# Weights streamed through TensorE from their last column to their first, with the PSUM output in the same order

## The reference

```python
x = x + 0.5 * swiglu(rms_norm(x, norm_ffn1_w), ffn1_w_gate, ffn1_w_up, ffn1_w_down)   # D_FF = 5632
x = x + head_group_mixer(rms_norm(x, norm_mix_w), w_in, attn_sinks, ret_gn_w, w_out)  # D_IN = 5376
x = x + 0.5 * swiglu(rms_norm(x, norm_ffn2_w), ffn2_w_gate, ffn2_w_up, ffn2_w_down)
return rms_norm(x, norm_final_w)

def swiglu(h, w_gate, w_up, w_down):
    return (jax.nn.silu(h @ w_gate) * (h @ w_up)) @ w_down
```

## Time and profile before

| | us |
|---|---|
| median of 3 runs | 1844.76 |
| lowest and highest run | 1844.43, 1845.06 |
| the profiled execution, own time | 1844.38 |
| its span, first to last instruction | 1842.6 |

### The profile page before, as it was taken

One profiled execution on the slowest core, in us unless ns is written; L12 is line 12 of the kernel. 1 busy time (PEld: TensorE's weight loads), 2 busy tenths in 40 slices (PEclk: granted clock), 3 DMA queues, 4 the chain that ended last, 5 costly groups with the idle time before them and its releaser, 6 DMA issues.

```text
span 1842.6 us, 23062 instructions
## 1 busy us (share of the span) xinstructions
PE 1830.3 (99%) x8570; PEld 1537.5 (83%) x8570; DVE 1045.0 (57%) x1087; ACT 832.0 (45%) x996; POOL 63.3 (3%) x59
## 2 busy tenths in 40 slices
PE   9999999999999999999999999999999999999998
PEld 7888888888888888999998888888888888888886
DVE  5565465455556557555557665555555556546546
ACT  7444443444444444555555455444444444444344
POOL 0000000000000000000009000000000000000000
PEclk9999999999999999999999999999999999999999
DMA  9565555555555555555555456555556565565552
GB/s 367 195 194 186 193 190 186 197 185 191 195 183 187 200 183 172 179 179 167 172 160 180 137 182 206 183 190 197 183 192 193 184 195 190 187 195 188 190 198 92
DMA packets 177345, 346.61 MB, mean 188 GB/s; under 512 B 6048, under 2 KB 31008, under 8 KB 177184
## 3 DMA queue, kind: packets, MB, share of 16 engines
q1 hardware_dynamic: 176880, 345.61, 57.0%
q10 hardware_dynamic: 432, 0.55, 0.1%
HBM read 344.04 MB, written 2.10 MB: 188 GB/s over the span
## 4 chain that ended last, share of the span: by engine, by line
PE 98%; DMA 0%; DVE 0%; issue 0%; ACT 0%; SPq 0%; POOLq 0%; POOL 0%; DVEq 0%
PE ps L325 32%; PE ps L327 32%; PE ps L326 32%; PE ps L352 2%; DMA raw<-in_g 0%; PE ps L477 0%; PE ps L561 0%; PE ps L572 0%; PE ps L490 0%; PE ps L446 0%; PE ps L445 0%; PE ps L444 0%; DVE x L895 0%; DVE proj L1082 0%; DVE w_lo L846 0%
## 5 line engine op out<-in xcount | busy, mean ns | idle before, releaser
L846 DVE TENSOR_TENSOR w_lo<-raw,w_hi 128x1024 fp32r<-128x1024 f32 x656 | 812.9, 1241 | 770.6 <-ACT w_hi L636 770.0
L636 ACT ACTIVATE w_hi<-raw 128x1024 fp32r<-128x1024 f32 x656 | 695.0, 1061 | 979.9 <-PE ps L327 969.7
L325 PE MATMUL ps<-w_hi,xT_hi 128*128 128x512 f32 (+1 forms) x1848 | 714.6, 387 | 0.9 <-DVE xT_lo L859 0.9
L327 PE MATMUL ps<-w_hi,xT_lo 128*128 128x512 f32 (+1 forms) x1848 | 710.1, 384 | 0.0
L326 PE MATMUL ps<-w_lo,xT_hi 128*128 128x512 f32 (+1 forms) x1848 | 709.9, 384 | 0.0
L325 PEld LDWEIGHTS ps<-w_hi,xT_hi 128*128 128x128 f32 x1848 | 347.1, 188 | 63.7 <-DVE xT_lo L859 1.3
L327 PEld LDWEIGHTS ps<-w_hi,xT_lo 128*128 128x128 f32 x1848 | 347.0, 188 | 63.0
L326 PEld LDWEIGHTS ps<-w_lo,xT_hi 128*128 128x128 f32 x1848 | 347.2, 188 | 61.6
L325 PE MATMUL ps<-w_hi,hT_hi 128*128 128x512 f32 x640 | 249.1, 389 | 0.0
L327 PE MATMUL ps<-w_hi,hT_lo 128*128 128x512 f32 x640 | 249.0, 389 | 0.0
L326 PE MATMUL ps<-w_lo,hT_hi 128*128 128x512 f32 x640 | 249.0, 389 | 0.0
(11 more groups left out here) (109 smaller groups left out, 514.0 us busy)
## 6 DMA issues: line engine op xcount, KB each, us to landing
raw<-in_u SPq DMA_DIRECT2D x88, 1024.0 KB, 5.1
raw<-in_d SPq DMA_DIRECT2D x88, 1024.0 KB, 4.9
raw<-in_g SPq DMA_DIRECT2D x87, 1024.0 KB, 5.1
raw<-in_w_in SPq DMA_DIRECT2D x48, 896.0 KB, 4.6
raw<-in_w_out SPq DMA_DIRECT2D x16, 1024.0 KB, 4.9
x<-in_x SPq DMA_DIRECT2D x4, 512.0 KB, 12.7
out<-proj SPq DMA_DIRECT2D x8, 256.0 KB, 2.4
proj<-in_xT SPq DMA_DIRECT2D x3, 512.0 KB, 9.8
```

The lines of the kernel that those rows point to most:

```text
L325: pe.matmul(out, xh, wh, start=first and j == 0, stop=False)
L327: mm = pe.matmul(out, xl, wh, start=False, stop=last and j == 1)
L636: act.activation(dst, raw[:, s, (k % 2) * HALF:(k % 2 + 1) * HALF], ACT.Copy).then_inc(hi_ready, 1)
L846: dve.tensor_tensor(w_lo[:, k % LEAD, :, :].rearrange(flat), raw[:, k // 2, (k % 2) * HALF:(k % 2 + 1) * HALF], f32(w_hi[:, k % LEAD, :, : ...
```

## The change

In `half`, all three products of every group read their weights with a column step of -1, from column width - 1 to column 0, and write their PSUM output with a step of -1 too. Column c of the weights still meets column c of the output. The number of instructions, the stationary operands, the addresses covered, the waits and the increments stay as they are. The products in `early_half` and in the last four halves, the transposes and the products of attention and retention keep their order.

```diff
                 for j in range(2):
                     for t in range(T):
-                        out = ps[:, bank + t, 0:width]
+                        out = ps[:, bank + t, 0:width][:, ::-1]
                         xh, xl = (a[:, kt + j, t * P:(t + 1) * P] for a in (a_hi, a_lo))
-                        wh, wl = (w[:, k % LEAD, j, 0:width] for w in (w_hi, w_lo))
+                        wh, wl = (w[:, k % LEAD, j, 0:width][:, ::-1] for w in (w_hi, w_lo))
                         pe.matmul(out, xh, wh, start=first and j == 0, stop=False)
                         pe.matmul(out, xh, wl, start=False, stop=False)
                         mm = pe.matmul(out, xl, wh, start=False, stop=last and j == 1)
```

## The result

The changed kernel takes 1890.62 us (median of 4 runs, 1890.46 to 1890.79) against 1844.81 us before: 1.0249 times as long, 95% interval 1.0231 to 1.0266, 45.8 us more. It is slower, and of the cases forecast it is the partial loss.

A forecast was written before the change was run, and what follows sets the result against it. The prediction took TensorE's products, 99% busy, as the bound. It summed 1844.38 + 0 for the profiled execution, 1844.8 us against the median of the runs, with an 8-in-10 range of 1838 to 3415 us.

The forecast's parts named there:

- the partial loss: Rival, chance 0.16: in `half`, weights' stream collides more with the stationary load, 39 us more at the `attT` price, 1883 us.
- What bounds the kernel: TensorE, busy 99%, never fed late; time is the count of products times the distance between their starts.
- Readers of PSUM, slots, waits: Readers of PSUM wait for a whole half, slots come free with its last product: cost nothing, same waits.
- I take no price: Reversed reads and writes in `half` cost 0 us, since aligned word pairs stay together: 1844.8 us, chance 0.37.
- Falling pairs not joined: Rival, chance 0.30: weights read or PSUM write in `half` handles single words, 1567 us more, 3411 us.
- The gain: Rival, chance 0.17: fewer collisions of weights' stream and stationary load, up to 10.7 ns a wide product, 87 us less, 1757.
- The change does nothing: Rival: a tool turns both reversed patterns back into rising ones, 1844.8 us; its chance is inside the 0.37 for no price.

The follow-up runs named there:

- pad_up: The kernel before, rising order kept, with 32 empty words ahead of `w_hi`: 1871.77 us, ratio 1.0146.
- att_pad: The kernel before with 64 empty words ahead of `attT` where it had 32: 1843.40 us, ratio 0.9993.
- both sets of shifts: Kernel before with rows of 16 equal products appended, stationary block or weights starting some words later: 32 words later 232.3 ns either way, unshifted 226.6.
- the third set: Kernel before with further rows of 16 equal products appended to test limits; plain float32, two records a product, took 429.1 ns each in both orders.
- the rows: Rows of 16 equal products appended behind the last product of the kernel before: 226.6 ns rising, 233.3 ns falling in the kernel's own form.

## Why the prediction was right or wrong

**What bounds the kernel.** Right. The count of products times the change of their distance gives the loss to 0.8 us, and a change of the distance passed through one to one.

**Readers of PSUM, slots, waits.** Right; no wait appeared, and the write order alone gives a ratio of 1.000.

**"I take no price", with the reason that every aligned pair of words is still used together.** This step failed. That pairs matter is true: reading every second column costs 453.7 ns. But using the pairs is not enough. In fp32r the stream's distance also depends on how its walk over stretches of up to 64 words stands to the place of the stationary block. The kernel before had 226.7 ns because it reads rising and because `xT`, `hT` and the weights lie alike modulo 64 words. The falling order pays 233.3 ns there, and none of the places tried for it gave less than 233.0. So the point number, 1844.8, missed by 45.8 us, and the time lies outside the 1841.0 to 1848.5 given for this case. The whole range, 1838 to 3415, held it only by its width: it reached that far for the sake of a rival that the runs refute.

**The partial loss**, at 0.16 the least likely of the four, is what happened, with the mechanism named there (stream and stationary load, as for `attT`) confirmed in one half: place counts, as pad_up, att_pad and both sets of shifts show. That falling collides more with the load is not confirmed: the falling stream stays at 233.4 ns when the load reads one word. Its size was 39 us forecast and 45.8 measured; the term was 5.2 ns a product from `attT` and is 6.6 ns on the wide ones, 4.0 on the narrow ones. That the size came near is in part luck: the 5.2 ns are the price of a place with a rising read, the 6.6 ns that of a falling read in the good place. What I held against it was a misreading: `xT` and `hT` have the same distance not because most places don't matter, but because both lie at the good one. Of the nine places of the block tried from 2 to 56 words off, none is as good.

**Falling pairs not joined**, 0.30, is refuted on both paths. Its price rested on a misreading: `retention_out` issues three products a head, and the six records of the earlier trace rows are two for each, as the third set shows for plain float32 (16 products, 32 records). So 0.844 ns a column is one record and a plain float32 product costs 1.69; that 432 ns came near the 453.7 of an unpaired read is luck. The strict reading of the Trainium skill's page "PSUM — Partial Sum Buffer" (Specifications), by which a pattern that isn't contiguous slows products, doesn't hold here: the trace shows 226.6 ns for a falling write and 226.7 for pairs with a step of four. The wording of the Trainium skill's "Advanced Engine Details and Errata" (Memory Cachelines) that asks for every two consecutive elements together agrees with these rows, though the same section has the strict rule too; a bf16 product that writes single columns costs 429.1 ns. The page "SBUF — State Buffer" of the Trainium skill (Specifications), by which two hits in a line of 16 bytes give full bandwidth, does not cover this read: falling fp32r makes four and loses 6.7 ns in the rows, and the measurement decides. For bf16 (215.9 ns both ways) it agrees.

**The gain**, 0.17, did not come. Of its 10.7 ns, 8.1 exist: a stream on one repeated column takes 218.6 ns. Falling order did not reach them. **The change does nothing** is excluded by the distances.

**Still open** is the layout behind the numbers: why a falling stream pays 20 ns over 512 / 2.4 = 213.3 even when the stationary load touches one word, why stretches of 64 words are the limit, why starts at 60 and 63 words are good and 62 is not, and why one kind of row can settle at two values (60 words: 226.7 and 228.1 ns; falling pieces of 32: 232.4 and 234.0). The runs show the dependence, not the circuit.

## What to carry to other kernels

When TensorE is never idle, read the distance between starts of neighbouring products and compare it across tiles: 227 against 232 ns for the same shape was a difference of place that could be had for 128 bytes of padding. For fp32r products with 512 columns keep the stream rising and put stationary and moving tiles at the same place modulo 64 words (256 bytes a partition); a tile allocated ahead of the weights can cost as much as a change of the loop. The order of output columns in PSUM was free in the fp32r orders tried, all of which kept neighbours in pairs.

## What the runs showed of the hardware

- A falling read of fp32r weights costs 233.3 ns for 512 columns against 226.7 rising; a falling write into PSUM costs nothing; bf16 and plain float32 products don't feel the order (215.9 ns, and two records of 429.1 ns, both ways).
- An fp32r read of every second column takes 453.7 ns, bf16 225.7; a bf16 product that writes every second column takes 429.1 ns, while plain float32 stays at its 429.1 ns a record.
- Rising and in place, products of 512, 384, 320 and 256 columns take 13.3 ns over columns / 2.4 (226.7, 173.3, 146.7, 120.0 ns); 496, 480 and 448 columns have 15.9 to 16.9 ns over. Falling, the excess is 20.0, 19.6, 20.0, 19.3, 17.6, 13.4 and 12.0 ns at 512, 496, 480, 448, 384, 320 and 256 columns. So the falling order costs 2.7 to 6.7 ns from 384 columns up and nothing at 320.
- A smaller stationary block doesn't speed up the stream behind it: with one column rising 231.3 ns, with 128 in the good place 226.7.
